# The last expert job is peeled off the loop, and its rows return by one-hot products in PSUM

## The reference

```python
def moe_swiglu(x, w_router, w_gate, w_up, w_down):
    logits = jnp.matmul(xt, w_router, ...)
    top_vals, top_idx = lax.top_k(logits, TOP_K)          # TOP_K = 2
    top_w = jax.nn.softmax(top_vals, axis=-1)
    ...
    for e in range(N_EXPERTS):                             # 8
        y = swiglu(xt, w_gate[e], w_up[e], w_down[e])      # 1024 -> 3584 -> 1024
        out = out + gates[:, e:e + 1] * y
```

## Time and profile before

| what | value |
|---|---|
| median of 3 runs | 1569.47 us (1568.69 to 1572.77) |
| the profiled execution, its own time | 1571.8 us |
| its span, first to last instruction | 1570.0 us |
| busy PE, DVE, ACT, POOL in the span | 1474.9, 1114.4, 943.8, 107.4 us |
| mean granted clock of PE | 0.967 of full speed |

### The profile page before, as it was taken

How to read it: one execution, slowest core, us unless ns; L and a number is a source line. 1 busy time by engine, 2 the same in 40 slices (tenths; PEclk the granted TensorE clock), 3 DMA queues, 4 the chain that set the end, 5 groups by cost and what they waited for, 6 DMA issues and landing times.

```text
span 1570.0 us, 18603 instructions
## 1 busy us (share of the span) xinstructions
PE 1474.9 (94%) x6691; PEld 1183.7 (75%) x6691; DVE 1114.4 (71%) x828; ACT 943.8 (60%) x796; POOL 107.4 (7%) x172
## 2 busy tenths in 40 slices
PE   5968899999999959999999999999999999999993
PEld 4544588888877648888888888888888888888882
DVE  1273554545332158998998999899898899889886
ACT  2042443434244437778778777778778778778773
POOL 3000100000100013002002001001001001002001
PEclk9967999999999969999999999999999999999997
DMA  8320756565343167999999999999999999999993
GB/s 274 124 73 0 279 168 210 164 209 166 113 153 122 40 228 266 399 373 384 381 373 375 386 368 378 393 360 380 385 371 376 394 366 382 386 364 377 389 370 140
DMA packets 178885, 448.88 MB, mean 286 GB/s; under 512 B 8800, under 2 KB 17056, under 8 KB 162720
## 3 DMA queue, kind: packets, MB, share of 16 engines
q1 hardware_dynamic: 174592, 433.65, 75.9%
q0 software_dynamic: 4256, 14.74, 2.4%
HBM read 442.04 MB, written 6.32 MB: 286 GB/s over the span
## 4 chain that ended last, share of the span: by engine, by line
PE 87%; DVE 5%; ACT 3%; issue 3%; DMA 1%; SPq 1%; POOL 1%; ACTq 0%; DVEq 0%; POOLq 0%
PE psum L541 23%; PE psum L543 23%; PE psum L542 23%; PE psum L409 5%; PE psum L420 4%; ACT w_hi L980 2%; PE psum L859 2%; PE psum L767 2%; DVE w_lo L1305 1%; PE psum L447 1%; DMA raw<-in_l_w_mem_kv 1%; PE psum L392 1%; DVE nmax L1256 1%; DVE reg_a L1273 0%; PE psum L375 0%
## 5 line engine op out<-in xcount | busy, mean ns | idle before, releaser
L1305 DVE TENSOR_TENSOR w_lo<-raw,w_hi 128x2048 fp32r<-128x2048 f32 x381 | 868.2, 2291 | 193.7 <-ACT w_hi L980 192.6
L980 ACT ACTIVATE w_hi<-raw 128x2048 fp32r<-128x2048 f32 x381 | 730.1, 1919 | 272.9 <-PE psum L543 272.8
L541 PE MATMUL psum<-w_hi,x_hi 128*128 128x512 f32 x1120 | 443.8, 396 | 11.6 <-DVE x_lo L1300 8.8
L543 PE MATMUL psum<-w_hi,x_lo 128*128 128x512 f32 x1120 | 437.6, 391 | 0.0
L542 PE MATMUL psum<-w_lo,x_hi 128*128 128x512 f32 x1120 | 437.0, 390 | 0.0
L541 PEld LDWEIGHTS psum<-w_hi,x_hi 128*128 128x128 f32 x1120 | 210.9, 188 | 57.2 <-DVE x_lo L1300 7.4
L543 PEld LDWEIGHTS psum<-w_hi,x_lo 128*128 128x128 f32 x1120 | 210.7, 188 | 45.0
L542 PEld LDWEIGHTS psum<-w_lo,x_hi 128*128 128x128 f32 x1120 | 211.0, 188 | 42.0
L541 PE MATMUL psum<-w_hi,h_hi 128*128 128x512 f32 x560 | 218.8, 391 | 0.0
L543 PE MATMUL psum<-w_hi,h_lo 128*128 128x512 f32 x560 | 217.9, 389 | 0.0
L542 PE MATMUL psum<-w_lo,h_hi 128*128 128x512 f32 x560 | 217.9, 389 | 0.0
(11 more groups left out here) (234 smaller groups left out, 865.1 us busy)
## 6 DMA issues: line engine op xcount, KB each, us to landing
raw<-in_l_w_gate SPq DMA_DIRECT2D x128, 1024.0 KB, 7.4
raw<-in_l_w_up SPq DMA_DIRECT2D x127, 1024.0 KB, 7.5
raw<-in_l_w_down SPq DMA_DIRECT2D x126, 1024.0 KB, 7.2
raw<-in_l_w_in SPq DMA_DIRECT2D x14, 1024.0 KB, 6.5
raw<-in_l_w_out SPq DMA_DIRECT2D x8, 1024.0 KB, 6.8
raw<-in_l_w_mem_kv SPq DMA_DIRECT2D x4, 1024.0 KB, 8.1
memb<-in_mem SPq DMA_DIRECT2D x2, 512.0 KB, 3.8
gains<-in_l_mem_g POOLq DMA_DIRECT2D x2, 512.0 KB, 7.6
```

The lines of the kernel that those rows point to most:

```text
L541: pe.matmul(out, x[0], w[0], start=first, stop=False, skip_group_check=True)
L543: return pe.matmul(out, x[1], w[0], start=False, stop=last, skip_group_check=True)
L980: act.activation(w_hi[:, m % CUT, :], raw[:, n % RAW, :], ACT.Copy).then_inc(hi_ok, 1)
L1305: dve.tensor_tensor(w_lo[:, m % CUT, :], raw[:, n % RAW, :], w_hi[:, m % CUT, :].bitcast(F32), ALU.subtract).then_inc(lo_ok, 1)
```

## The change

1. The body of the loop becomes a function `expert_job(j, last)` on PE, ACT and DVE. The loops run over `n_jobs - 1` jobs, and a second copy of the body follows each of them for the last job. That copy leaves out `next_rows`, the cutting of pieces for a next job, and the rounding of the next rows. POOL's loop is one shorter, so the last job has no scatter.
2. DVE builds `pick_last` ahead of the loops: for each token a one-hot row that says which row of the last job is its own. PE turns it during the last job, ACT copies it out as `pickT`, and after the last job PE multiplies `pickT` by `y_sb`, four matmuls (two token tiles by two halves) into banks 2 to 5.
3. SP waits for the scatter of the last job but one, and loads `part0` and `part1` behind the last weights of the last job. DVE adds them ahead of its scaling of `y_sb`, and adds the products from PSUM on top later.
4. Rows of `ys` that belong to the last job are never written by a scatter, so `ys` is cleared early: DVE sets a tile to zero, and SP writes it four times (512 KB each) behind the first six weight loads. DVE waits for that ahead of the first post-norm.

```diff
@@ PE
-            with pe.Fori(0, n_jobs) as j:
+            def expert_job(j, last):
...
                     expert_rows("g", b)
+                    if last and b == 0:
+                        pe.wait_ge(pick_last_ok, 1)
+                        begin(("pickT",), 6)
+                        for tt in range(NT):
+                            ins = pe.transpose(bank(6, tt * P, (tt + 1) * P), pick_last[:, tt, :], ident[:, :])
+                        end(ins, ("pickT",))
...
-                            next_rows()
+                            if not last:
+                                next_rows()
...
+                pe.wait_ge(*bk.empty(("pickT",)))
                 for hf in range(2):
-                    pe.wait_ge(*bk.empty(("gather", hf), j))
+                    pe.wait_ge(*bk.empty(("y", hf), j))
+                for tt in range(NT):
+                    for hf in range(2):
+                        jbegin(("back", tt, hf), 2 + 2 * tt + hf)
+                        ins = pe.matmul(bank(2 + 2 * tt + hf), pickT[:, tt, :], y_sb[:, hf * 512:(hf + 1) * 512],
+                                        start=True, stop=True)
+                        end(ins, ("back", tt, hf))
+
+            with pe.Fori(0, n_jobs - 1) as j:
+                expert_job(j, False)
...
+            expert_job(n_jobs - 1, True)
@@ ACT, in the job
-                    if (kind, b, half) == ("d", NB - 2, 1):
+                    if last and (kind, b, half) == ("d", 0, 0):
+                        copy(("pickT",), pickT, bank(6, 0, 256).rearrange("p (t s) -> p t s", t=NT))
+                    if (kind, b, half) == ("d", NB - 2, 1) and not last:
...
-                    cut_high1(j, i + CUT)
+                    if not last or i + CUT < NPC:
+                        cut_high1(j, i + CUT)
@@ DVE, at the start, ahead of the first post-norm, and ahead of the loop
+            dve.memset(zeros, 0.0).then_inc(zeros_ok, 1)
...
+            dve.wait_ge(cleared, 16 * (SLOTS // P))
             post_norm(POST0, 0, ("mix", 0), xn)
...
+            link(dve.tensor_scalar(last_f[:, :], job_f[:, 3:4], -1.0, -float(CAP), ALU.add, ALU.mult))
+            link(dve.tensor_scalar(row_f[:, :, :], row_f[:, :, :], last_f[:, 0:1], None, ALU.add))
+            for tt in range(NT):
+                ins = dve.tensor_scalar(pick_last[:, tt, :], iota_s[:, :], row_f[:, tt, 0:1], None, ALU.is_equal)
+            link(ins)
+            for tt in range(NT):
+                ins = dve.scalar_tensor_tensor(out=pick_last[:, tt, :], in0=iota_s[:, :], scalar=row_f[:, tt, 1:2],
+                                               in1=pick_last[:, tt, :], op0=ALU.is_equal, op1=ALU.add)
+            ins.then_inc(pick_last_ok, 1)
@@ DVE, in the job and behind it
+                    if last and i == NPC - 1:
+                        for tt in range(NT):
+                            dve.wait_ge(parts_in[tt], 32)
+                            dve.tensor_tensor(part0[:, tt, :], part0[:, tt, :], part1[:, tt, :], ALU.add)\
+                                .then_inc(whole, 1)
...
-            for tt in range(NT):
-                dve.wait_ge(parts_in[tt], 32)
-                dve.tensor_tensor(part0[:, tt, :], part0[:, tt, :], part1[:, tt, :], ALU.add).then_inc(whole, 1)
...
+            for tt in range(NT):
+                dve.wait_ge(whole, tt + 1)
+                for hf in range(2):
+                    dve.wait_ge(*bk.full(("back", tt, hf), n_jobs - 1))
+                dve.tensor_tensor(part0[:, tt, :], part0[:, tt, :],
+                                  psum[:, 2 + 2 * tt:4 + 2 * tt, :].rearrange("p a b -> p (a b)"), ALU.add)\
+                    .then_inc(whole, 1)
@@ SP
+            def clear_rows():
+
+                sp.wait_ge(zeros_ok, 1)
+                for q in range(SLOTS // P):
+                    sp.dma_start(ys[q * P:(q + 1) * P, :], zeros).then_inc(cleared, 16)
...
             for n, src in enumerate(loads):
+                if n == RAW:
+                    clear_rows()
...
-            for m in range(CUT):
-                expert_load(0, m, cut_of(n_jobs, m))
-            sp.wait_ge(moved, 16 * n_jobs + TABLED)
+            sp.wait_ge(moved, 16 * (n_jobs - 1) + TABLED)
```

More of the change, by code:

```diff
@@ L179, in trunk @@
         row_i = sb("row_i", [P, NT, 2], I32)
+        last_f = sb("last_f", [P, 1])
         job_f = sb("job_f", [P, 4])
@@ L217, in trunk @@
         x_rows = work[:, 3072:4096]
+        pick_last = work[:, 2816:3072].rearrange("p (t s) -> p t s", t=NT)
+        pickT = work[:, 2048:2304].rearrange("p (t s) -> p t s", t=NT)
+        zeros = w_lo[:, 0, 0:D].bitcast(F32)
         picked_hi, picked_lo = x_hi[:, :, 0:CAP], x_lo[:, :, 0:CAP]
@@ L268, in trunk @@
         rows_in, index_ok = sem("rows_in"), sem("index_ok")
+        zeros_ok, cleared, pick_last_ok = sem("zeros_ok"), sem("cleared"), sem("pick_last_ok")
         parts_in = [sem(f"parts{tt}_in") for tt in range(NT)]
@@ L907, in _ @@
                 expert_down(NB - 1, 1)
-                for hf in range(2):
-                    pe.wait_ge(*bk.empty(("gather", hf), j))
+                if not last:
+                    for hf in range(2):
+                        pe.wait_ge(*bk.empty(("gather", hf), j))
+                    return
+                pe.wait_ge(*bk.empty(("pickT",)))
+                for hf in range(2):
+                    pe.wait_ge(*bk.empty(("y", hf), j))
[7 more added lines that the diff above has]
+                expert_job(j, False)
             assert tuple(bk.count[b] - base[b] for b in range(8)) == TURN
             assert n_used[0] - used_before == USED_TURN
+            bk.count = list(base)
+            n_used[0] = used_before
+            expert_job(n_jobs - 1, True)
         @block.scalar
@@ L1161, in _, with expert_job @@
             n_jobs = act.value_load(job_i[0:1, 3:4], min_val=NE, max_val=MAX_JOBS)
-            with act.Fori(0, n_jobs) as j:
+            def expert_job(j, last):
                 def full(label):
@@ L1183, in _ @@
                             .then_inc(bk.empty_sem(("y", 0)), 1)
-                    cut_high1(j, i + CUT)
+                    if not last or i + CUT < NPC:
+                        cut_high1(j, i + CUT)
+            with act.Fori(0, n_jobs - 1) as j:
+                expert_job(j, False)
+            expert_job(n_jobs - 1, True)
             for tt in range(NT):
-                act.wait_ge(whole, tt + 1)
+                act.wait_ge(whole, NT + tt + 1)
                 square_sum(FPOST1, tt, part1[:, tt, :], part0[:, tt, :])
@@ L1552, in _, with expert_job @@
             dve.tensor_copy(row_i[:, :, :], row_f[:, :, :]).then_inc(entries_ok, 1)
+            link(dve.tensor_scalar(last_f[:, :], job_f[:, 3:4], -1.0, -float(CAP), ALU.add, ALU.mult))
[7 more added lines that the diff above has]
+            ins.then_inc(pick_last_ok, 1)
             dve.wait_ge(tables_ok, 1)
             n_jobs = dve.value_load(job_i[0:1, 3:4], min_val=NE, max_val=MAX_JOBS)
-            with dve.Fori(0, n_jobs) as j:
+            parts_before = n_part[0]
+            def expert_job(j, last):
                 def full(label):
@@ L1579, in _ @@
                             .then_inc(bk.empty_sem(("y", 1)), 1)
-                    cut_rest(i + CUT, i + CUT, NPC * j + (NPC + i + CUT + 1))
-            for tt in range(NT):
-                dve.wait_ge(parts_in[tt], 32)
-                dve.tensor_tensor(part0[:, tt, :], part0[:, tt, :], part1[:, tt, :], ALU.add).then_inc(whole, 1)
+                    if not last or i + CUT < NPC:
+                        cut_rest(i + CUT, i + CUT, NPC * j + (NPC + i + CUT + 1))
+            with dve.Fori(0, n_jobs - 1) as j:
+                expert_job(j, False)
+            n_part[0] = parts_before
+            expert_job(n_jobs - 1, True)
+            for tt in range(NT):
+                dve.wait_ge(whole, tt + 1)
+                for hf in range(2):
+                    dve.wait_ge(*bk.full(("back", tt, hf), n_jobs - 1))
+                dve.tensor_tensor(part0[:, tt, :], part0[:, tt, :],
+                                  psum[:, 2 + 2 * tt:4 + 2 * tt, :].rearrange("p a b -> p (a b)"), ALU.add)\
+                    .then_inc(whole, 1)
             for tt in range(NT):
@@ L1666, in expert_rows @@
                 n_jobs = pool.value_load(job_i[0:1, 3:4], min_val=NE, max_val=MAX_JOBS)
-                with pool.Fori(0, n_jobs) as j:
+                pool.wait_ge(cleared, 16 * (SLOTS // P))
+                with pool.Fori(0, n_jobs - 1) as j:
                     pool.wait_ge(*bk.full(("gather", 1), j - 1))
```

## The result

| | median | runs |
|---|---|---|
| before | 1569.08 us | 1568.45 to 1572.77, 4 runs |
| changed | 1557.60 us | 1556.63 to 1558.30, 4 runs |

The ratio is 0.9917, 95% interval 0.9903 to 0.9931: 13.0 us less of 1569.47, or 1556.4 us on the scale of the prediction. Two later comparisons of the same kernel gave 0.9895 (0.9878 to 0.9911) and 0.9913 (0.9899 to 0.9926).

The account below looks back on a forecast made before the run. TensorE, busy 94% of the span, bounds the jobs; behind them lies a serial 26.45 us tail. Savings of 10.1 (tail), 0.65 (transposes) and 0.4 (function tables) sum to 11.2 us: 1569.47 to 1558.3 us, range 1556.8 to 1562.5.

Parts of the forecast that it names:

- steps 1 and 2: Tail: VectorE starts scaling bank 1 after 0.50 us and takes 0.74; TensorE then waits 0.50; sum 1.74 us.
- Step 3: Tail: four plain float32 products on TensorE, 1.90 us for the first token tile and 1.74 for the second.
- the rival of a fallen clock: TensorE's clock falls to 1.2 GHz before the tail's products, costing 3.5 us, 1561.8 us in all; chance 0.05.
- Step 4: Tail: 0.20 us from TensorE's end to VectorE's start, then a 1.25 us sum with one operand in PSUM.
- Step 5: Tail: 3.50 us from the second sum's end to the second scaling by the root, GpSimd held up once more.
- TensorE in the last job: Last job: 8 next-row transposes (0.87 us) go and 2 one-hot-row transposes (0.22) come; 0.65 us saved.
- The term for the function tables: Start of last job: the copy has no ScalarE table loads, so TensorE loses its wait for a cut; 0.4 us saved.
- Parts, pick_last, clearing: Loading and adding parts in the last job, building one-hot rows, and early clearing writes: each cost 0, clearing up to 2 us.
- The rival with a chance of 0.13: ScalarE and VectorE must fetch code behind the loop only on leaving it, costing 1.6 to 5.2 us; chance 0.13.
- the one of starved code: TensorE waits for each instruction block of the last job's copy, adding 17 to 33 us, 1575 to 1591; chance 0.03.

Follow-up runs that it names:

- peel_only: The kernel before with the last job in its own copy without unused loads, cuts and next-rows transposes, scatter and parts loads kept; 1564.76 us, ratio 0.9964.
- halves: The changed kernel, but TensorE multiplies both token tiles by the first scaled half while VectorE scales the second; 1555.89 us, ratio 0.9911 to before.
- two_tables: The changed kernel with one extra one-column exponential on ScalarE ahead of the last job, giving two table loads there; 1558.21 us, ratio 0.9910 to before.

## Why the prediction was off by more than its range allowed

The direction, the mechanism and the order of the size were right. 1558.3 us was forecast, and the measured ratio gives 1556.4 us, 0.4 us below the low end of the range. The forecast saving of 11.2 us was 1.25 short of what the last job and the tail gave: 0.96 in the tail, 0.34 in the wait behind the table loads, and 0.05 the other way in the transposes and by rounding. A further 0.6 us is in no stage. Point by point:

- **The tail, steps 1 and 2: this is the step that failed.** I took "0.50 us for a wait with a register operation behind it" from ScalarE, and used it for VectorE and for TensorE. ScalarE's 0.50 us was no latency. The row ahead of that scaling in the timeline of before, which I had not weighed:

```profile
1540.86 1.92 ACT L980 ACTIVATE w_hi<-raw 128x2048 fp32r<-128x2048 f32 x1 [0.80 <-PE psum L543]
```

  ScalarE was at a cut until 1542.78, and the scaling started as it ended (the two records overlap by 0.09 us). With the cut gone it starts 1538.40 - 1538.28 = 0.12 us after its bank is full, VectorE 0.14 us (1539.78 - 1539.64), and TensorE 0.13 us after VectorE (1540.66 - 1540.53). That is 0.73 us too much in the sum. For step 2 the forecast named 0.09 as the lower bound and took the upper one; for step 1 it had no bound at all.
- **Step 3**, the products: 3.69 us for 8 records, 3.64 forecast. Right, and the granted clock was 1.00 from 1539.6 to 1544.4 us, so the rival of a fallen clock did not happen.
- **Step 4**, 0.20 to VectorE: 0.12 (1540.66 + 3.69 = 1544.35 to 1544.47). The sum from PSUM took 1.22, not 1.25.
- **Step 5**, 3.50 from the second sum to the second scaling: 3.51 (1545.69 to 1549.20). GpSimd was held up in both of its operations, 0.57 and 1.54 us. The mechanism was forecast, but no row gave the 0.33 that it adds to the 3.17 of before, so the fit to 0.01 is luck. Store: 3.26 for 3.46. Sum of the tail: 15.4, where I had 16.3.
- **TensorE in the last job**: the transposes, forecast at 0.65, gave 0.89 - 0.27 = 0.62. The term for the function tables was mis-sized: 0.4 was the idle time that the waits view lists, and the wait cost TensorE 0.74. Together 1.36 for 1.05.
- **Parts, pick_last, clearing**: all hidden, as forecast. The parts' loads start at 1520.1 us and VectorE sums at 1536.13 without a wait. Two experiments on the clearing and one on the sums found no cost. VectorE stood idle for 1.0 us ahead of the first cut, where it had 2.47.
- **Code behind the loop**: five more packets on the first queue (28 for 23), TensorE waits for nothing in the last job but the new wait. The rival with a chance of 0.13 and the one of starved code did not happen.
- **From trace to median, and the range.** 11.2 us were forecast, 12.45 us are in last job and tail, and the times gave 13.0 us and, in the later comparisons, 13.7 and 16.5. By the stages alone the time would be 1569.47 - 12.45 = 1557.0 us, inside the range; the further 0.6 us put it outside. The stages ahead of the jobs move by up to 7 us between profiles of these kernels, and I had put nothing for that into the range: its low end went by the latencies alone. The 0.6 us are well inside the interval of 0.9903 to 0.9931. But 12.45 us would be a ratio of 0.9921, and the interval of the second comparison, with four runs, ends at 0.9911. All three ratios lie on the same side, and the mean of all 14 runs of the changed kernel is 13.8 us below that of the 26 runs of before taken beside them. The change may be worth about 1 us more than its stages show; no profile has a stage for it, and that stays open.

## What to carry to other kernels

Before a gap between two engines is read as a latency, look at what the second engine ran in that gap: if its last operation ends as the next starts, the gap is a queue, and it goes when that operation goes. When a loop is peeled, the saving is in what the last pass does for a next pass that never comes, and in whom these leftovers hold up; here that was 4.9 of 12.45 us. A short wait of TensorE costs more than the idle time listed for it; measure it from start to start of the matmuls, here 0.7 us for a listed 0.41. For a change of under 1%, cut both traces at marks that all kernels share and compare stage by stage: the spans of the changed kernel alone ran from 1555.0 to 1558.8 us, nearly all of it ahead of the jobs.

## What the runs showed of the hardware

- GpSimd's one-column operation took 2.17 us while VectorE subtracted 128x2048 elements, and 0.19 us with VectorE idle (peel_only). The same with the two operations of the root: 0.18 and 0.58 us free, up to 1.24 (before) and 1.54 us beside VectorE's work on 128x1024 elements. The 2.17 us and the 1.16 us of halves ended 0.06 and 0.05 us after VectorE's operation did, as if held until then. In this tail a small operation on GpSimd was priced by what VectorE did meanwhile.
- A branch not taken at the end of a hardware loop, into a second copy of some 540 matmuls of TensorE, cost no time: 5 packets of instructions more came, one between 1400 and 1430 us and four behind it, while the weights kept the transfer engines 0.92 busy, and TensorE had no wait in that job. The Trainium skill, "Runtime: NRT & Kernel Launch", section "Instruction fetch mechanics", says that fetching is sequential and ahead of use; the trace agrees.
- The wait for the first weights varied from 3.8 to 6.8 us between executions of one kernel, and TensorE's mean granted clock from 10 to 180 us from 0.84 to 0.87; over all twelve profiles it went up to 0.88.
- ScalarE's two loads of a function table in each pass of the loop, 1.28 us each, cost TensorE 0.74 us in the last pass of the kernel before, and 0.56 us when two_tables put them back.
